# A frequency-domain step that adds up in PSUM, is multiplied from PSUM, and a new order around it

## The reference

```
z_f = rfft(z, n=1024); y = irfft(z_f * k_f, n=1024)[:, :512]
z = gate * (y + d_bias * z)
```

## Time and profile before

| what | value |
|---|---|
| median of three runs | 1854.79 us (1847.06 to 1858.77) |
| profiled execution | 1853.79 us, its span 1852.4 us |
| busy: TensorE, VectorE, ScalarE, GpSimd | 95%, 53%, 33%, 39% |
| mean granted TensorE clock | 0.983 |
| the Hyena steps | about 1204 to 1415 us of the span |

### The profile page before, as it was taken

How to read it: one execution, slowest core, us unless ns; L and a number is a source line. 1 busy time by engine, 2 the same in 40 slices (tenths; PEclk the granted TensorE clock), 3 DMA queues, 4 the chain that set the end, 5 groups by cost and what they waited for, 6 DMA issues and landing times.

```text
span 1852.4 us, 19432 instructions
## 1 busy us (share of the span) xinstructions
PE 1768.9 (95%) x7732; PEld 1401.9 (76%) x7732; DVE 977.5 (53%) x1362; ACT 620.3 (33%) x872; POOL 727.5 (39%) x331
## 2 busy tenths in 40 slices
PE   5899999999998999999999999999998999999997
PEld 2556888888876666778888788778887788888785
DVE  8787433321354755564444213698896754444124
ACT  1525222222243543253333212533232433333222
POOL 1122444444433130434444444365554344444442
PEclk9999999999999999999999999999999999999998
DMA  9963423232222020223232332422222222323232
GB/s 348 340 225 114 131 96 100 94 98 96 91 77 78 24 68 1 80 80 103 91 102 91 99 95 91 184 89 80 91 91 91 80 91 94 101 93 100 91 93 78
DMA packets 54340, 197.43 MB, mean 107 GB/s; under 512 B 6216, under 2 KB 6664, under 8 KB 52393
## 3 DMA queue, kind: packets, MB, share of 16 engines
q1 hardware_dynamic: 52584, 190.05, 31.0%
q10 hardware_dynamic: 1666, 6.14, 0.9%
HBM read 183.58 MB, written 12.58 MB: 106 GB/s over the span
## 4 chain that ended last, share of the span: by engine, by line
PE 80%; DVE 13%; issue 2%; ACT 2%; DMA 1%; POOL 1%; SPq 0%; DVEq 0%; ACTq 0%
PE ps L488 25%; PE ps L490 25%; PE ps L489 25%; PE ps L534 1%; PE ps L856 1%; DVE x_residual L2142 1%; POOL w_lo L1502 1%; DVE x_residual L2133 1%; DVE n_values L1848 1%; DMA decay<-in_decay 1%; DVE filter_taps L1740 1%; DVE x_residual L2129 1%; DVE x_residual L2128 1%; DVE x_residual L2132 1%; PE ps L630 1%
## 5 line engine op out<-in xcount | busy, mean ns | idle before, releaser
L1502 POOL TENSOR_TENSOR w_lo<-w_raw,w_hi 128x1024 fp32r<-128x1024 f32 x244 | 595.1, 2440 | 909.3 <-ACT w_hi L1048 858.0
L488 PE MATMUL ps<-act_hi,w_hi 128*128 128x512 f32 x1348 | 532.4, 395 | 18.7 <-POOL w_lo L1502 7.9
L490 PE MATMUL ps<-act_hi,w_lo 128*128 128x512 f32 x1348 | 528.3, 392 | 0.0
L489 PE MATMUL ps<-act_lo,w_hi 128*128 128x512 f32 x1348 | 527.8, 392 | 0.0
L1048 ACT ACTIVATE w_hi<-w_raw 128x1024 fp32r<-128x1024 f32 x248 | 262.7, 1060 | 791.3 <-PE ps L490 783.1
L488 PEld LDWEIGHTS ps<-act_hi,w_hi 128*128 128x128 f32 x1348 | 254.8, 189 | 77.3 <-POOL w_lo L1502 7.8
L489 PEld LDWEIGHTS ps<-act_lo,w_hi 128*128 128x128 f32 x1348 | 255.1, 189 | 53.7 <-issue 1.2
L490 PEld LDWEIGHTS ps<-act_hi,w_lo 128*128 128x128 f32 x1348 | 254.7, 189 | 53.4
L488 PE MATMUL ps<-f_hidden_hi,w_hi 128*128 128x512 f32 x528 | 208.8, 395 | 1.9 <-POOL w_lo L1502 1.9
L489 PE MATMUL ps<-f_hidden_lo,w_hi 128*128 128x512 f32 x528 | 206.6, 391 | 0.0
L490 PE MATMUL ps<-f_hidden_hi,w_lo 128*128 128x512 f32 x528 | 206.4, 391 | 0.0
(11 more groups left out here) (261 smaller groups left out, 2330.9 us busy)
## 6 DMA issues: line engine op xcount, KB each, us to landing
w_raw<-in_w_stream SPq DMA_DIRECT2D x258, 512.0 KB, 3.5
mod_ring<-in_mod_t SPq DMA_DIRECT2D x18, 512.0 KB, 8.6
x_tokens<-in_mod_t SPq DMA_DIRECT2D x18, 512.0 KB, 4.9
spectra<-filter_spectra SPq DMA_DIRECT2D x16, 512.0 KB, 6.9
hy_filter<-spectra SPq DMA_DIRECT2D x8, 1024.0 KB, 4.8
mod_ring_more<-in_mod_t SPq DMA_DIRECT2D x12, 512.0 KB, 10.4
x_residual<-in_xT ACTq DMA_DIRECT2D x8, 256.0 KB, 10.4
x_tokens<-in_x_tokens SPq DMA_DIRECT2D x1, 2048.0 KB, 11.9
```

The lines of the kernel that those rows point to most:

```text
L488: PE.matmul(o, lh, rh, start=start, stop=False, **kw)
L489: PE.matmul(o, lh, rl, start=False, stop=False, **kw)
L490: return PE.matmul(o, ll, rh, start=False, stop=stop, **kw)
L1502: GP.tensor_tensor(low, B.WR[:, c % 2, :], f32(high), ALU.subtract).then_inc(S.w_lo, 1)
```

## The change

The forward step takes only two banks (`freq_bank`: 4 and 5 for f = 0, 2 and 3 for f = 1). Both kinds' even times are multiplied first; ScalarE copies each even bank to SBUF (`hy_even`), and then the odd times are added onto the same bank, which then holds even plus odd. VectorE's `products` makes the minus half as twice the copy less the bank, and multiplies the bank itself with the filter, four times; `combine` is the two remaining sums of the plus half. The minus half of steps 0 to 6 stays on GpSimd; that of step 7 is `last_minus` on VectorE, and GpSimd waits there for all of `prod_lo` before it goes on with chunk base + 24. TensorE's order is as it was, but its waits differ. ScalarE's and VectorE's orders are new.

```diff
@@ -912,20 +913,26 @@
             PE.wait_ge(S.z_lo, 4 * half + 4)
             if s == 0:
                 PE.wait_ge(S.tables_lo, 1)
-            elif half == 0 or f == 0:
-
-                PE.wait_ge(S.minus_part, 2 * s)
-                PE.wait_ge(S.plus_part, 2 * s)
-            else:
-
-                PE.wait_ge(S.gated, 4 * half)
+            elif half and f:
+
+                PE.wait_ge(S.gated, 4 * half - 2)
+            elif half:
+
+                PE.wait_ge(S.freq_read, s - 1)
+                if half > 1:
+                    PE.wait_ge(S.gated, 4 * half - 4)
             zh, zl = B.ZS[half]
-            for kind in range(2):
-                for parity in range(2):
+            for parity in range(2):
+                for kind in range(2):
+                    if parity:
+                        PE.wait_ge(S.even_part, 2 * s + kind + 1)
                     for k in range(2):
                         b = dft_block(kind, parity, k, f)
-                        ins = mm3(ps[:, 2 + 2 * kind + parity, :], B.FH[:, b, :], B.FL[:, b, :],
-                                  zh[:, 2 * parity + k, :], zl[:, 2 * parity + k, :], k == 0, k == 1)
+                        ins = mm3(ps[:, freq_bank(f, kind), :], B.FH[:, b, :], B.FL[:, b, :],
+                                  zh[:, 2 * parity + k, :], zl[:, 2 * parity + k, :], (parity, k) == (0, 0), k == 1,
+                                  skip_group_check=True)
+                    if parity == 0:
+                        ins.then_inc(S.freq_even, 1)
             ins.then_inc(S.freq, 1)
...
         def invert(half, f):
@@ -933,8 +940,7 @@
             s = 2 * half + f
             if f == 0:
 
-                PE.wait_ge(S.minus_part, min(4 * half + 6, 16))
-                PE.wait_ge(S.plus_part, min(4 * half + 6, 16))
+                PE.wait_ge(S.freq_read, min(2 * half + 3, 8))
                 if half == 0:
                     PE.wait_ge(S.tables_lo, 2)
             PE.wait_ge(S.prod_lo, 4 * s + 4)
...
+def freq_bank(f, kind):
+
+    return 4 - 2 * f + kind
...
+        def even_parts(half, f):
             s = 2 * half + f
-            SC.wait_ge(S.freq, s + 1)
-            if s:
-                SC.wait_ge(S.plus_part, 2 * s)
-            SC.activation(B.OD[:, 0, :], ps[:, 3, :], ACT.Copy).then_inc(S.odd_part, 1)
-            SC.activation(B.OD[:, 1, :], ps[:, 5, :], ACT.Copy).then_inc(S.odd_part, 1)
-
-        def prod_hi(half, f):
+            for kind in range(2):
+                SC.wait_ge(S.freq_even, 2 * s + kind + 1)
+                if s:
+                    SC.wait_ge(S.minus_part, 2 * s - 1 + kind)
+                SC.activation(B.EV[:, kind, :], ps[:, freq_bank(f, kind), :], ACT.Copy).then_inc(S.even_part, 1)
+
+        def prod_hi(half, f, first=0, last=4):
             s = 2 * half + f
             high, _ = product_slot(B, s)
-            for i, (part, dst) in enumerate(PRODUCT_SUMS):
+            for i, (part, dst) in list(enumerate(PRODUCT_SUMS))[first:last]:
                 SC.wait_ge(S.prod, 4 * s + i + 1)
                 if i == 0 and s == 0:
 
...
         split_and_mid(5, 7)
-        odd_parts(0, 0)
+        even_parts(0, 0)
         split_and_mid(7, 9)
         z_hi(1, 0)
+        even_parts(0, 1)
         prod_hi(0, 0)
-        odd_parts(0, 1)
         split_and_mid(9, 10)
         z_hi(1, 1)
         split_and_mid(10, 11)
-        odd_parts(1, 0)
-        split_and_mid(11, 12)
+        even_parts(1, 0)
         prod_hi(0, 1)
-        split_and_mid(12, 14)
-        prod_hi(1, 0)
-        odd_parts(1, 1)
+        split_and_mid(11, 14)
+        prod_hi(1, 0, 0, 2)
+        even_parts(1, 1)
+        prod_hi(1, 0, 2, 4)
         z_hi(2, 0)
         split_and_mid(14, 15)
         z_hi(2, 1)
         split_and_mid(15, 16)
+        even_parts(2, 0)
         prod_hi(1, 1)
-        odd_parts(2, 0)
         w_hi(base + 18)
         prod_hi(2, 0)
         mid(16)
         split_and_mid(17, 18)
-        odd_parts(2, 1)
+        even_parts(2, 1)
         z_hi(3, 0)
         split_and_mid(18, 19)
         z_hi(3, 1)
         split_and_mid(19, 20)
+        even_parts(3, 0)
         prod_hi(2, 1)
-        odd_parts(3, 0)
         split_and_mid(20, 22)
-        prod_hi(3, 0)
-        odd_parts(3, 1)
+        prod_hi(3, 0, 0, 2)
+        even_parts(3, 1)
+        prod_hi(3, 0, 2, 4)
         split_and_mid(22, 24)
...
@@ -1626,9 +1638,9 @@
         w_lo(base + 22)
         minus_sin()
         w_lo(base + 23)
-        minus_cos(3, 1)
+
+        GP.wait_ge(S.prod_lo, 32)
         w_lo(base + 24)
-        minus_sin()
...
@@ -2106,39 +2118,52 @@
                 VE.tensor_tensor(low[:, q, :], ps[:, turn_bank(half, q), :], f32(high[:, q, :]),
                                  ALU.subtract).then_inc(S.z_lo, 1)
 
-        def butterfly(half, f):
+        def products(half, f):
+
             s = 2 * half + f
-            VE.wait_ge(S.odd_part, 2 * s + 2)
+            cos, sin = ps[:, freq_bank(f, 0), :], ps[:, freq_bank(f, 1), :]
+            VE.wait_ge(S.freq, s + 1)
             if s:
                 VE.wait_ge(S.prod_hi, 4 * s)
                 VE.wait_ge(S.v_sin, s)
                 VE.wait_ge(S.prod_lo, 4 * s)
             else:
                 VE.wait_ge(S.x_spilled, 16 * KD)
-            VE.tensor_tensor(X[:, 2, :], ps[:, 2, :], B.OD[:, 0, :], ALU.subtract).then_inc(S.minus_part, 1)
-            VE.tensor_tensor(X[:, 3, :], ps[:, 4, :], B.OD[:, 1, :], ALU.subtract).then_inc(S.minus_part, 1)
-            VE.tensor_tensor(X[:, 0, :], ps[:, 2, :], B.OD[:, 0, :], ALU.add).then_inc(S.plus_part, 1)
-            VE.tensor_tensor(X[:, 1, :], ps[:, 4, :], B.OD[:, 1, :], ALU.add).then_inc(S.plus_part, 1)
-
-        def plus_cos(half, f):
+            for kind, bank in enumerate((cos, sin)):
+                VE.scalar_tensor_tensor(out=X[:, 2 + kind, :], in0=B.EV[:, kind, :], scalar=2.0, in1=bank,
+                                        op0=ALU.mult, op1=ALU.subtract).then_inc(S.minus_part, 1)
+            VE.wait_ge(S.filter_in, 16 * (s + 1))
+            own.mark(VE.tensor_tensor(X[:, 4, :], cos, B.KS[:, 0, :], ALU.mult))
+            own.mark(VE.tensor_tensor(X[:, 5, :], sin, B.KS[:, 2, :], ALU.mult))
+            own.mark(VE.tensor_tensor(X[:, 0, :], cos, B.KS[:, 2, :], ALU.mult))
+            VE.tensor_tensor(X[:, 1, :], sin, B.KS[:, 0, :], ALU.mult).then_inc(S.freq_read, 1)
+
+        def combine(half, f):
             s = 2 * half + f
-            VE.wait_ge(S.plus_part, 2 * s + 2)
-            VE.wait_ge(S.filter_in, 16 * (s + 1))
-            own.mark(VE.tensor_tensor(X[:, 4, :], X[:, 0, :], B.KS[:, 0, :], ALU.mult))
-            after(own.mark(VE.tensor_tensor(X[:, 5, :], X[:, 1, :], B.KS[:, 2, :], ALU.mult)))
-            own.mark(VE.tensor_tensor(X[:, 4, :], X[:, 4, :], X[:, 5, :], ALU.subtract))
-
-        def plus_sin():
-            own.mark(VE.tensor_tensor(X[:, 0, :], X[:, 0, :], B.KS[:, 2, :], ALU.mult))
-            after(own.mark(VE.tensor_tensor(X[:, 1, :], X[:, 1, :], B.KS[:, 0, :], ALU.mult)))
-            VE.tensor_tensor(X[:, 0, :], X[:, 0, :], X[:, 1, :], ALU.add).then_inc(S.filter_read, 1)
+            VE.wait_ge(S.freq_read, s + 1)
+            after(own.n)
+            VE.tensor_tensor(X[:, 4, :], X[:, 4, :], X[:, 5, :], ALU.subtract).then_inc(S.plus_made, 1)
+            VE.tensor_tensor(X[:, 0, :], X[:, 0, :], X[:, 1, :], ALU.add).then_inc(S.plus_made, 1)
+
+        def last_minus():
+
+            VE.wait_ge(S.minus_part, 16)
+            own.mark(VE.tensor_tensor(X[:, 6, :], X[:, 2, :], B.KS[:, 1, :], ALU.mult))
+            after(own.mark(VE.tensor_tensor(X[:, 7, :], X[:, 3, :], B.KS[:, 3, :], ALU.mult)))
+            VE.tensor_tensor(X[:, 6, :], X[:, 6, :], X[:, 7, :], ALU.subtract).then_inc(S.v_cos, 1)
+            own.mark(VE.tensor_tensor(X[:, 2, :], X[:, 2, :], B.KS[:, 3, :], ALU.mult))
+            after(own.mark(VE.tensor_tensor(X[:, 3, :], X[:, 3, :], B.KS[:, 1, :], ALU.mult)))
+            VE.tensor_tensor(X[:, 2, :], X[:, 2, :], X[:, 3, :], ALU.add).then_inc(S.v_sin, 1)
 
         def sums(half, f, low=0, high=4):
             s = 2 * half + f
-            VE.wait_ge(S.filter_read, s + 1)
+            VE.wait_ge(S.plus_made, 2 * s + 1 + high // 3)
             for dst, x1, x2, op, v in ((1, 4, 6, ALU.add, S.v_cos), (5, 4, 6, ALU.subtract, S.v_cos),
                                        (3, 0, 2, ALU.add, S.v_sin), (7, 0, 2, ALU.subtract, S.v_sin))[low:high]:
                 VE.wait_ge(v, s + 1)
+                if dst == 1:
+
+                    VE.wait_ge(S.plus_made, 2 * s + 2)
                 VE.tensor_tensor(X[:, dst, :], X[:, x1, :], X[:, x2, :], op).then_inc(S.prod, 1)
...
                              ALU.mult).then_inc(S.gated, 1)
 
-        def gates(half):
-            for m in range(4):
+        def gates(half, low=0, high=4):
+            for m in range(low, high):
                 gate(half, m)
 
...
-        butterfly(0, 0)
-        plus_cos(0, 0)
+        products(0, 0)
         branches(7, 8)
```

(91 more changed lines are left out.)

## The result

The changed kernel takes 1836.74 us (median of 7 runs, 1832.46 to 1847.02), the kernel before 1854.60 beside it (7 runs, 1847.06 to 1858.77): a ratio of 0.9923, 95% interval 0.9899 to 0.9946. The forecast median was 1839.3, with a range of its own of 1835 to 1843 and 0.58 of the chance on a change within 1%; both hold. The profiled execution of after took 1842.17 us, with a span of 1840.9; forecast 1838.3.

The account below looks back on a forecast made before the run. TensorE holds 80% of the chain of waits, so only its gaps pay: -15.6 (gaps) - 5.4 (slow clock) + 1.5 + 2.5 (new stalls) + 1.5 (their clock) = -15.5 us, a median of 1839.3 us, range 1835 to 1843.

Parts of the forecast that it names:

- six gaps and their slow clock: TensorE's six waits for VectorE between about 1190 and 1420 us: 15.6 idle plus 5.4 slow clock, 21.0 us won.
- stall (a): New wait ahead of branch product 13, as branches(11) now stands behind products(1,0): 0.9 to 2.0 us, taken as 1.5.
- stall (b): New wait ahead of invert(1,0) for products(2,0), now after four full reads: 2.5 us, plus 1.5 of slow clock.
- PSUM products: VectorE's four filter products a step read PSUM and escape turns with GpSimd: 0.60 to 0.70 us each.
- The hand-over: ScalarE's copies inside eight forward steps cost 0; its rival, TensorE standing at them, gives 1867 us, chance 0.07.
- The last step: Ahead of invert(3,1): prod_lo(3,1) ends 15.6 us after forward(3,1), 1.0 before need, so the 5.54 gap goes.
- F: Start of forward(2,0), from which the walk to invert(1,0) counts: products end at F + 13.7, TensorE ready at F + 11.2.
- The slow clock: TensorE partly at 1.2 GHz behind gaps: 5.4 us won at three old gaps, 1.5 added at stall (b).
- no new stall: Rival: VectorE wins its turns and both new waits are met; the whole 21.0 us won, 1833.8, chance 0.25.
- displaced waits: Rival: slack at forward(1,0), turn(2,1), invert(3,1) or invert(2,0) is lost too, giving back 7.7 us: 1847, chance 0.20.
- products do not escape: Rival: filter products still take turns with GpSimd, 1.7 us each; some 11 us gained less 5 of stalls: 1849, chance 0.03.

Follow-up runs that it names:

- second profile: The changed kernel run again without edits, on one chip with e9: stage 209.44 us, ratio 0.9944 to the kernel before.
- e4: Changed kernel, but forward(1,1) and (3,1) wait for all four gates, not the two of their banks: stage 210.21 us against 207.87.
- e3: Changed kernel, but VectorE copies two banks out of PSUM and the four filter products read the SBUF copies: stage 228.05 us against 207.87.
- e2: Changed kernel with the forward step's loops exchanged, each odd half directly behind its own kind's even half: stage 218.60 us against 207.87.
- e5: Changed kernel, but GpSimd no longer waits for prod_lo(3,1) before w_lo of the first two hy_out chunks: stage 212.74 us against 207.87.
- e7: Changed kernel with minus_sin(1,1) ahead of w_lo of base + 16 on GpSimd: stage 206.07 us against 207.87.
- e8: Changed kernel with branches(15, 16) behind products(2, 0) on VectorE: stage 206.33 us against 207.87.
- e9: Changed kernel with branches(11, 12) ahead of products(1, 0), minus_sin(1,1) ahead of w_lo, branches(15, 16) behind products(2, 0): median 1831.18 us, ratio 0.9890 to before.

## Why the prediction was right

By its own steps. The forecast counted gaps by their idle figures; the measured column is in start-to-start lengths, and each idle figure is 0.16 less than what the gap costs from start to start (branch product 10 takes 7.69 instead of 5.46 ahead of the gap of 2.07), since the end of the product before it is modelled late. That alone is 1.0 us over six gaps:

| Step | Forecast | Measured |
|---|---|---|
| six gaps and their slow clock, won | 21.0 | 22.4 |
| stall (a) | 1.5, no slow clock | 2.28 + 0.16, + 1.8 slow clock |
| stall (b) | 2.5, + 1.5 slow clock | 2.13 + 0.16, no slow clock (1.5 in the second profile) |
| stage | -15.5 | -15.8 (second profile -14.2) |

The mechanism held, but that the sum came within 0.3 us is luck: 1.4 more was won than forecast, (a) cost 2.7 more with its slow clock, and (b) 1.6 less without one. The second profile, the same instructions, misses by 1.3.

**The gaps.** All six went, and the margins lie near those of the walk. z_lo(1,0) ends 6.7 us before turn(1,1) (forecast 6.7). z_lo(1,1) ends at 1241.1 and forward(1,0) starts at 1241.78: margin 0.6 (forecast 0.5). z_lo(2,0) ends at 1290.9 against turn(2,1) at 1291.24: 0.3 (forecast 0.2). e4 isolates the wait for two gates instead of four: 0.88 of the gates' 2.44 and 1.34. How much of the other gaps the new operations closed and how much the new order isn't shown: no run has one without the other. e3 shows only that with products from SBUF the new order doesn't hold them.

**PSUM products** take 0.68, 0.60 apart, beside GpSimd, as said, and VectorE's busy time fell by 33 us where I counted on over 22. e3 takes the PSUM inputs away and adds two copies a step; together these two cost more than the whole gain. The rival on it came to 1849, with some gain left; e3 leaves none and is 4.4 us longer in the stage than before. Its four gaps say why: the rival let the stalls grow by 5, but VectorE's lateness used up the margins at forward(1,0) and turn(2,1), and one at turn(3,1) that I had not named, as well as growing stall (b), each with a slow clock.

**The hand-over** costs nothing covered: ScalarE's two copies at forward(2,0), the first behind a split and a mid,

```profile
1299.38 0.59 ACT L1421 ACTIVATE hy_even<-ps 128x512 f32<-128x512 f32 x1
1300.61 0.60 ACT L1421 ACTIVATE hy_even<-ps 128x512 f32<-128x512 f32 x1 [0.64 <-PE ps L491]
```

end at 1299.97 and 1301.21; the odd half of the first kind is due at 1297.65 + 2 x 1.37 = 1300.39: 0.4 us of margin (forecast 0.5). Five other steps have the same 0.4, forward(0,1) among them, where 0.6 was forecast. The rival was 16.5 us away, at the price of e2.

**The last step** was E + 15.6 for the end of prod_lo(3,1). E is 1379.8 here, where forward(3,1)'s last product ends, and ScalarE and VectorE show

```profile
1391.71 0.67 ACT L1383 ACTIVATE hy_branches<-ps,params 128x512 f32<-128x512 f32 x1
1392.28 2.18 ACT L1433 ACTIVATE hy_turned_hi<-x_residual 128x512 fp32r<-128x512 f32 x4
```

```profile
1392.93 2.50 DVE L2174 TENSOR_TENSOR hy_turned_lo<-x_residual,hy_turned_hi 128x512 fp32r<-128x512 f32 x4 [0.63 <-ACT hy_turned_hi L1433]
```

an end at 1395.4, E + 15.6, and mid(23) at E + 12.5, both as written. The w_lo of hy_out's first two chunks end at 1400.3, E + 20.5, and hy_out starts at 1402.05 without waiting.

**Stall (a)** came out past the upper end of its bounds (0.9 to 2.0) by 0.3. Counted from forward(1,0), v_sin(0,1) was put at +7.6 to +9.0 and landed at +9.1: w_lo started at +1.5 where the walk had +1.06, 0.2 of it because GpSimd's minus_cos(0,1) ran until then and the rest in hand-overs; it took 2.84, not 2.40, and two minus operations 1.75, because VectorE's combine and sums, now earlier, ran into them. I took a mean where the trace of before showed both prices; the end at which both engines meet was the right one, since the change moves VectorE's SBUF work towards GpSimd's.

Another part of the miss is a term that the prediction put at nothing: the filter load of this step. It was to be in, after 4.8 us, by the end of the two minus operations. SP issues it once v_sin(0,1) is there, at 1250.99, and it lands 5.60 us later; the first filter product starts at 1256.61, 0.2 later than straight behind them. In e5 the load took 6.25, and VectorE's timeline names it:

```profile
1249.92 0.69 DVE L2134 TENSOR_TENSOR x_residual<-ps,hy_filter 128x512 f32<-128x512 f32 x1 [0.77 <-DMA hy_filter<-spectra]
```

Over the seven profiles that have both this order and stall (a) the stall is 2.20 to 2.94, the product comes 0.12 to 0.85 late, and the stall less that is 2.07 to 2.11 each time. So VectorE's queue makes 2.1 us of stall (a), and the load all of what varies.

**Stall (b)**: TensorE was ready at F + 11.1 (forecast 11.2), products ended at F + 13.2 (13.7). But what made the sums late was named wrongly in part: not w_lo ahead of v_sin, since e7 took that away and the gap stayed, but sums against any GpSimd work, and taps 15 behind them, which e8 removed for 1.4 us. That sums meeting GpSimd cost the rest is read from the traces; no run holds GpSimd still there.

**The slow clock** was one spell, in the sum and in the profile, at the other gap. Its place was luck; its count was too, as the second profile has two. Between the rivals the runs decide as follows: "no new stall" is e9, not this order; "displaced waits" and "products do not escape" didn't occur.

## What to carry to other kernels

Where GpSimd has a steady load, give VectorE's operations one PSUM input, even at the price of another hand-over inside the matmul group, and put the other kind's products between; count SBUF-only VectorE work at the price of the GpSimd instruction that it meets. Where such work must be quick once, hold GpSimd still for it. When a chain gets shorter, look again at what stands behind the last wait in each queue: two pairs of taps moved past a neighbour gave, with a third move that did nothing, another 5.7 us of the stage against the first profile of the change, 7.3 against the second.

## What the runs showed that was not expected

**Gap length doesn't decide the clock between 2 and 3 us.** Over the twelve profiles of this study, before's among them, 19 gaps of TensorE in this stage were between 2.04 and 2.94 us long. Behind 11 of them the clock went from 2.4 to 1.2 GHz for a while and cost 1.5 to 1.8 us, behind 8 it did not. It did behind 2.09 (e3), 2.13 (e4) and 2.14 (e5); it did not behind 2.53 (e4) and 2.94 (e5):

```profile
1255.25:1262.45 7.20, 7.20 (x38) 1.00 0.25 75
...
1305.00:1312.20 7.20, 7.20 (x47) 0.76 0.23 65
```

These are the windows behind e4's gaps of 2.53 and 2.13. In this stage all five gaps of 3.66 to 5.54 cost clock, and none of 1.54 or less did, nor did e2's sixteen of 0.69 to 0.84. The rest of the same traces, which no edit touches, warns against making rules of these lengths: a gap of 2.35 near 569 us was followed by slow clock in all twelve profiles, one of 2.87 near 744 us in seven, one of 2.99 near 665 us in five, and over the 7.2 us behind one of 1.51 near 1820 us, where only small products follow, the mean granted clock was 0.56 to 0.76 in all twelve. What decides stays open. A forecast should price such a gap with a little over half of 1.6 us and widen its range by the rest.

**An uncovered copy costs more than itself.** ScalarE's copy of a bank takes 0.60, the idle time is 0.69 to 0.84, and the step grows by 1.0 for each (16.5 over 16).

**Copying out of PSUM first would have been the wrong advice here.** A filter product takes 0.68 from PSUM, and so do the copy and, from SBUF with GpSimd held still, a product of last_minus. The Trainium skill (VectorE: DVE Perf Modes, section on the TRN2 errata) charges a PSUM source more. After and e3 show no surcharge at 128 x 512 in fp32, and in e3 copying first and multiplying in SBUF beside GpSimd costs 20.2 us of the stage. The advice to copy, which the prediction cites together with the charge, stands in that page's section "Rules for kernel authors".
